# Level masks moved from GpSimd to VectorE, and reciprocal roots computed by a power instruction on GpSimd, in a two-layer encoder trunk

## The chip, the cores and the metric

The kernel runs on one core of one Trainium2 chip. The metric is the device time of one launch in microseconds (us); the time given is the median of three runs. The core has the matrix engine TensorE (PE in the profile), VectorE (DVE), ScalarE (ACT), GpSimd (POOL), and SyncE (SP), which here only issues DMAs. All engines run their own instruction streams and meet at semaphores.

## What is computed

Two layers over one sequence of 256 tokens of width 2048, all in fp32. Every layer is a token mixer and a SwiGLU feed-forward part, each closed by a residual sum and a LayerNorm. The mixer of layer 0 has two halves, RWKV-7 (16 heads of 64, both directions) and gated linear attention (GLA, 4 heads); that of layer 1 is differential attention. Reciprocal square roots stand in five places:

```python
def _layer_norm(x, g, b, eps=1e-5):
    mu = mean(x); var = mean(square(x - mu))
    return (x - mu) * rsqrt(var + eps) * g + b        # 4 times over D=2048; and per RWKV head (eps 64e-5)

def _rms_norm(x, g, eps=1e-5):                        # GLA output (256 wide), attention output (128 wide)
    return x * rsqrt(mean(x*x) + eps) * g

def _l2norm(t, eps=1e-12):                            # RWKV: kk = _l2norm(heads(k * k_k)), per token and head
    return t / maximum(sqrt(sum(t*t)), eps)

def step(S, inp):                                     # RWKV-7, one token; the kernel does it in chunks of 64
    r_t, w_t, k_t, v_t, kk_t, a_t = inp
    sa = -einsum(S, kk_t)
    S = S * w_t + sa * (kk_t * a_t) + v_t * k_t
    return S, einsum(S, r_t)
```

## The kernel before, in words

The large projections multiply in split fp32: ScalarE copies a weight tile to a rounded high part (`high`), VectorE subtracts for the low part (`low`), and TensorE runs three matmuls for each product. One wait counter for each pair of producer and consumer sets the order; there is no scheduler, each engine's block is written out by hand.

The RWKV half runs over 8 pairs of heads (`PAIRS`), one after the other, the sequence cut into 4 chunks of 64 in both directions (8 units). For each pair, the inverse of a triangular 64 x 64 matrix for each unit is built by doubling, in levels `lv` 1 to 5. At each level TensorE makes three products (`L1984`): Q = V * C into PSUM `py`, then the new V into `pt` and the new W into `pa`. ScalarE copies the upper 64 partitions of each into SBUF and VectorE the lower 64: Q into `R_Qbd` (L1338, L1648), V into `R_Vbd` (L1342, L1652), W into `R_wc` (L1346, L1656). TensorE's next product waits for both copies. C of a level is the score matrix `R_G` times that level's 0/1 mask, written by `level(eng, lv)` (L250, L255), in two instructions of 64 x 512. VectorE does levels 0 and 1, GpSimd levels 2 to 5, each as soon as the buffer `R_C[lv % 2]` is free (`q_done` two levels back). After the levels comes a serial chain over 4 chunks, then `pair_done`.

Work for the next pair is spread into the gaps of the levels. The tables `ACT_AT`, `DVE_AT`, `PE_AT` say which numbered piece of `next_act`, `next_dve`, `next_pe` stands at which level and point (0 is behind the Q copy, 1 behind the V copy, 2 behind the W copy). VectorE's piece 3 clamps the sum of squares of kk into `R_sh[:, 1]` (L1578, 128 x 256, semaphore `ss_clamped`). ScalarE turns it into the reciprocal root with Ln (piece 3, L1287) and Exp with scale -0.5 (piece 4, L1290), semaphore `rn_ready`, for which VectorE's piece 4 waits at L1587. Ln, Exp and Sigmoid do not share a loaded table here, so a table load stands ahead of each change.

The tail of a pair, a LayerNorm over each head, lies at the start of the next pair: VectorE computes four variances (`ys_var`, L1691), ScalarE does Ln and Exp on 128 x 4 (`act_tail`, L1301, L1303), VectorE normalises (`normed`, L1599) and later finishes (`finish`, L1606 to L1611). GpSimd, per pair: zeroes `R_UV`, copies the next z columns (`next_z`), copies `R_Kbd` and `R_Rbd`, does the four masks, then `next_factors`. The other reciprocal roots are L1405/L1407 (each GLA head, 128 x 2), L1472/L1474 (attention, 128 x 32, once) and `end_act` (L669/L671, 128 x 2, four times).

## Time and profile before

| | us |
|---|---|
| median of 3 runs | 3432.48 (3430.94 to 3436.76) |
| the profiled execution | 3431.72 |
| its span | 3429.9 |
| PE busy | 2875.8 (84%) |
| DVE busy | 2180.7 (64%) |
| ACT busy | 1216.6 (35%) |
| POOL busy | 364.4 (11%) |
| chain that ended last, by engine | PE 63%, issue 16%, DVE 13%, DVEq 4%, ACT 2%, ACTq 1% |

The profile gives the busy time of each engine, the groups of instructions by line (L255 is line 255 of the kernel), the idle time ahead of each group with what ended it, and single instructions in order of time. The projections and feed-forward parts take most of the span; the RWKV pairs lie between about 452 and 1040 us, the GLA heads after them to 1166 us, the attention heads between 2392 and 2509 us.

### The profile page before, as it was taken

The numbers are of one execution on the slowest core, as the hardware profiler recorded it, in microseconds if no ns is written. First come the engines' busy times: TensorE is split into PE (matmuls) and PEld (weight loads), VectorE is DVE, ScalarE is ACT, GpSimd is POOL, SyncE is SP. The second block draws the span as 40 slices with busy tenths as digits, with TensorE's granted clock in tenths as the row PEclk, the third lists the DMA queues.
The fourth block names the chain that finished last, engine by engine and source line by source line (L and its number), as shares of the span: only waits on it lengthen the run. The fifth ranks groups of instructions, "written<-read, shape, count | busy, mean of one in ns | idle before, by whom it ended". The sixth has DMA issues, their size and how long they took to land.

```text
span 3429.9 us, 43071 instructions
## 1 busy us (share of the span) xinstructions
PE 2875.8 (84%) x16704; PEld 2381.3 (69%) x16704; DVE 2180.7 (64%) x2308; ACT 1216.6 (35%) x1398; POOL 364.4 (11%) x405
## 2 busy tenths in 40 slices
PE   1799857776773588999999996999678899999996
PEld 1588746666662476888888885887556788888885
DVE  7768355666655656777778778743666555555557
ACT  0333333333323343333333332433543333333332
POOL 0000042333220002000000002011801000000001
PEclk9999967667675698999999997999778999999998
DMA  9799410110004454888678873955034555555552
GB/s 357 277 348 357 140 32 29 38 45 28 28 1 160 172 164 154 325 311 318 258 298 329 304 280 114 356 179 171 0 111 135 175 193 184 195 188 191 187 192 86
DMA packets 256765, 635.48 MB, mean 185 GB/s; under 512 B 10238, under 2 KB 17204, under 8 KB 234292
## 3 DMA queue, kind: packets, MB, share of 16 engines
q1 hardware_dynamic: 250530, 621.77, 51.0%
q10 hardware_dynamic: 6162, 12.72, 1.0%
q8 instruction: 48, 0.79, 0.1%
q14 instruction: 25, 0.20, 0.0%
HBM read 632.35 MB, written 2.10 MB: 185 GB/s over the span
## 4 chain that ended last, share of the span: by engine, by line
PE 63%; issue 16%; DVE 13%; DVEq 4%; ACT 2%; ACTq 1%; DMA 0%; POOL 0%; POOLq 0%; SPq 0%
PE pa L552 9%; PE pa L554 9%; PE pa L553 9%; PE pb L552 5%; PE pb L554 5%; PE pb L553 5%; PE py L552 4%; PE py L554 4%; PE py L553 4%; DVE s_wl L462 2%; PE pt L1984 1%; DVE s_wide L501 1%; DVE s_htl L607 1%; PE pa L1984 1%; PE pt L511 1%
## 5 line engine op out<-in xcount | busy, mean ns | idle before, releaser
L462 DVE TENSOR_TENSOR s_wl<-s_raw,s_wh 128x2048 fp32r<-128x2048 f32 (+1 forms) x396 | 919.4, 2323 | 709.5 <-ACT s_wh L457 707.3
L457 ACT ACTIVATE s_wh<-s_raw 128x2048 fp32r<-128x2048 f32 (+1 forms) x396 | 757.8, 1915 | 1300.7 <-PE pa L554 638.9
L552 PE MATMUL pa<-s_wh,s_hth 128*128 128x512 f32 (+1 forms) x1760 | 703.3, 400 | 48.9 <-DVE s_wl L462 33.0
L553 PE MATMUL pa<-s_wl,s_hth 128*128 128x512 f32 (+1 forms) x1760 | 695.4, 395 | 0.0
L554 PE MATMUL pa<-s_wh,s_htl 128*128 128x512 f32 (+1 forms) x1760 | 694.5, 395 | 0.0
L552 PEld LDWEIGHTS pa<-s_wh,s_hth 128*128 128x128 f32 x1760 | 337.9, 192 | 125.7 <-issue 46.3
L554 PEld LDWEIGHTS pa<-s_wh,s_htl 128*128 128x128 f32 x1760 | 337.1, 192 | 71.4
L553 PEld LDWEIGHTS pa<-s_wl,s_hth 128*128 128x128 f32 x1760 | 337.9, 192 | 68.5
L501 DVE SCALAR_TENSOR_TENSOR s_wide<-s_adaw,s_silu_c,s_wide 128x2048 f32<-128x2048 f32 x150 | 352.7, 2351 | 4.2 <-issue 3.0
L552 PE MATMUL py<-s_wh,s_guh 128*128 128x512 f32 x704 | 278.1, 395 | 13.3 <-DVE s_ysum L913 10.8
L554 PE MATMUL py<-s_wh,s_gul 128*128 128x512 f32 x704 | 276.0, 392 | 0.0
L553 PE MATMUL py<-s_wl,s_guh 128*128 128x512 f32 x704 | 275.8, 392 | 0.0
L552 PE MATMUL pb<-s_wh,s_hth 128*128 128x512 f32 x704 | 274.5, 390 | 0.0
L553 PE MATMUL pb<-s_wl,s_hth 128*128 128x512 f32 x704 | 273.9, 389 | 0.0
L554 PE MATMUL pb<-s_wh,s_htl 128*128 128x512 f32 x704 | 273.9, 389 | 0.0
L552 PEld LDWEIGHTS py<-s_wh,s_guh 128*128 128x128 f32 x704 | 133.5, 190 | 46.8 <-DVE s_wl L462 8.4
L554 PEld LDWEIGHTS py<-s_wh,s_gul 128*128 128x128 f32 x704 | 133.3, 189 | 28.2
L553 PEld LDWEIGHTS py<-s_wl,s_guh 128*128 128x128 f32 x704 | 133.6, 190 | 27.5
L552 PEld LDWEIGHTS pb<-s_wh,s_hth 128*128 128x128 f32 x704 | 132.2, 188 | 27.5 <-DVE s_wl L462 0.3
L554 PEld LDWEIGHTS pb<-s_wh,s_htl 128*128 128x128 f32 x704 | 132.1, 188 | 27.4
L553 PEld LDWEIGHTS pb<-s_wl,s_hth 128*128 128x128 f32 x704 | 132.2, 188 | 27.2
L719 POOL TENSOR_TENSOR s_xt<-s_xt,s_lng 128x2048 f32<-128x2048 f32 x6 | 28.9, 4830 | 805.6 <-PE py L580 792.8
(339 smaller groups left out, 3166.8 us busy)
## 6 DMA issues: line engine op xcount, KB each, us to landing
s_raw<-in_ffn_w_in SPq DMA_DIRECT2D x176, 1024.0 KB, 5.2
...
```

Source lines behind the costliest of these rows:

```text
L457: act.activation(wh[:, s % 2, :, 0:width], raw[:, s, :, 0:width], ACT.Copy).then_inc(hi_done, 1)
L462: dve.tensor_tensor(wl[:, s % 2, :, 0:width], raw[:, s, :, 0:width], wh[:, s % 2, :, 0:width].bitcast(F32), ALU.subtract).then_inc(lo_done, 1)
L501: dve.scalar_tensor_tensor(wide[:], adaw[:, slot], silu_c[:, bass.ds(k, 1)], wide[:], ALU.mult, ALU.add).then_inc(ada_step, 1)
L511: mm = pe.matmul(bank[:, m:m + 1], wide[:, m * P:(m + 1) * P], ones[:, 0:1], start=(m == 0), stop=True, skip_group_check=True)
L552: pe.matmul(o, a_hi, w_hi, start=start and k == 0, stop=False)
L553: pe.matmul(o, a_hi, w_lo, start=False, stop=False)
L554: mm = pe.matmul(o, a_lo, w_hi, start=False, stop=stop and k == UK - 1)
L607: dve.tensor_tensor(htl[:, 2 * g:2 * g + 2, :], htmp[:, g % 2], hth[:, 2 * g:2 * g + 2, :].bitcast(F32), ALU.subtract).then_inc(h_lo, 1)
L719: pool.tensor_tensor(xt[:, i], xt[:, i], lng[:], ALU.mult)
L1984: mm = pe.matmul(bank[r, h, u * CH:(u + 1) * CH], lhs(u, h), rhs(u, h), start=(start or (start is None and u == 0)), stop=True, skip_group ...
```

## The change

1. `level` is called for levels 2 to 5 by VectorE, between its Q copy and its V copy, and no longer by GpSimd.
2. Every reciprocal root is one `tensor_tensor` with `ALU.pow` on GpSimd, its second operand a column that holds -0.5, broadcast. ScalarE's Ln and Exp for it go, with the pieces 3 and 4 of `next_act`; the pieces left are numbered anew in `ACT_AT`.
3. The factor 65536 inside Ln and the factor 256 behind it go, so that L1587 becomes a plain product.

```diff
--- before.py
+++ after.py
@@ -250,8 +250,6 @@
         def level(eng, lv):
 
             for h, rows_ in enumerate((slice(0, CH), slice(CH, P))):
-                if h and eng is nc.gpsimd:
-                    eng.drain()
                 ins = eng.tensor_tensor(
                     R_C[rows_, lv % 2].rearrange("p (d c) n -> p d c n", d=2),
                     R_G[rows_, h, :, 0:CH].rearrange("p (d c) n -> p d c n", d=2),
@@ -277,7 +275,7 @@
         IN_PARTS = {c: 4 * (c - 1) if c < 5 else 4 * (c - 2) for c in (1, 2, 3, 4, 6, 7, 8, 9)}
 
 
-        ACT_AT = {(1, 2): 1, (2, 0): 2, (3, 2): 3, (4, 0): 4, (4, 1): 5, (4, 2): 6}
+        ACT_AT = {(1, 2): 1, (2, 0): 2, (4, 1): 3, (4, 2): 4}
         DVE_AT = {(1, 0): 0, (1, 2): 1, (2, 2): 2, (3, 0): 3, (4, 1): 4}
         PE_AT = {1: 1, 2: 2}
 
@@ -664,12 +662,6 @@
             act.dma_start(lng[:], ln_g[n // 2, n % 2].partition_broadcast(P)).then_inc(ln_in, 16)
             act.dma_start(lnb[:], ln_b[n // 2, n % 2].partition_broadcast(P)).then_inc(ln_in, 16)
 
-        def end_act(act, n):
-            act.wait_ge(end_var, n + 1)
-            act.activation(small[:, 36:38], small[:, 34:36], ACT.Ln)
-            act.drain()
-            act.activation(small[:, 38:40], small[:, 36:38], ACT.Exp, scale=-0.5).then_inc(end_rstd, 1)
-
         stats = small[:, 40:88].rearrange("p (i c s) -> p i c s", i=NT, s=6)
 
         def end_block(dve, n, q):
@@ -1098,6 +1090,8 @@
         @block.gpsimd
         def _(pool):
             pool.memset(rows[:], 0.0).then_inc(rows_zero, 1)
+            pool.memset(small[:, 95:96], -0.5)
+            half_neg = small[:, 95:96]
 
             pool.wait_ge(unit_done, 2 + 4 * ABC)
             for tile in (R_Kbd, R_Rbd, R_Wbd, R_Qbd, R_Vbd):
@@ -1122,6 +1116,12 @@
             def units(tile, rows_, at):
                 return tile[rows_, :, at:at + CH]
             full, top, low_half = slice(0, P), slice(0, CH), slice(CH, P)
+
+            def next_norm(n):
+
+                pool.wait_ge(ss_clamped, n + 1)
+                pool.sem_inc(passed, 1)
+                pool.tensor_tensor(R_sh[:, 1], R_sh[:, 1], half_neg.to_broadcast((P, SEQ)), ALU.pow).then_inc(rn_ready, 1)
 
             def next_factors(n):
 
@@ -1136,9 +1136,17 @@
                     pool.tensor_tensor(units(R_AB, rows_, at_b), both(R_rk[rows_, 1]), R_e2[rows_], ALU.mult)
                 pool.drain().then_inc(ab_ready, 1)
 
-            def pool_pair(t, more):
+            def pool_tail(t):
+
+                pool.wait_ge(ys_var, t + 1)
+                pool.sem_inc(passed, 1)
+                pool.tensor_tensor(small[:, 24:28], small[:, 16:20], half_neg.to_broadcast((P, 4)), ALU.pow).then_inc(ys_rstd, 1)
+
+            def pool_pair(t, more, tail=True):
                 pool.wait_ge(pair_done, t + 1)
                 pool.sem_inc(passed, 1)
+                if tail:
+                    pool_tail(t - 1)
                 pool.memset(R_UV[:], 0.0)
                 pool.drain().then_inc(init_ready, 1)
                 if more:
@@ -1151,20 +1159,19 @@
                 pool.tensor_copy(R_Kbd[CH:P, :, CH:P], R_KR[CH:P, :, 0:CH])
                 pool.tensor_copy(R_Rbd[CH:P, :, CH:P], R_KR[CH:P, :, CH:P])
                 pool.drain().then_inc(krbd_ready, 1)
-                for lv in range(2, LEVELS):
-                    pool.wait_ge(first_ready if lv == 2 else q_done, t + 1 if lv == 2 else t * (LEVELS - 1) + lv - 2)
-                    pool.sem_inc(passed, 1)
-                    level(pool, lv)
-                    pool.drain().then_inc(c_ready, 1)
                 if more:
+                    next_norm(t + 1)
                     pool.wait_ge(ab_turned, t + 1)
                     pool.sem_inc(passed, 1)
                     next_factors(t + 1)
             next_z(0)
+            next_norm(0)
             next_factors(0)
-            with pool.Fori(0, PAIRS - 1) as t:
+            pool_pair(0, True, False)
+            with pool.Fori(1, PAIRS - 1) as t:
                 pool_pair(t, True)
             pool_pair(PAIRS - 1, False)
+            pool_tail(PAIRS - 1)
             pool.wait_ge(tail_done, PAIRS)
             pool.sem_inc(passed, 1)
 
@@ -1180,16 +1187,29 @@
                 pool.drain().then_inc(gv_ready, 1)
             gla_qk(0)
             gla_v(0)
+            def gla_norm(n):
+                pool.wait_ge(g_var, n)
+                pool.sem_inc(passed, 1)
+                pool.tensor_tensor(small[:, 32:34], small[:, 28:30], half_neg.to_broadcast((P, 2)), ALU.pow).then_inc(g_rstd, 1)
             with pool.Fori(1, GH) as n:
                 pool.wait_ge(g_turned, n)
                 pool.sem_inc(passed, 1)
                 gla_qk(n)
                 pool.wait_ge(g_o, n)
                 pool.sem_inc(passed, 1)
+                gla_norm(n)
                 gla_v(n)
+            gla_norm(GH)
+
+            def end_norm(n):
+
+                pool.wait_ge(end_var, n + 1)
+                pool.tensor_tensor(small[:, 38:40], small[:, 34:36], half_neg.to_broadcast((P, 2)), ALU.pow).then_inc(end_rstd, 1)
+            end_norm(0)
             pool.wait_ge(x_ready, 2)
             pool.memset(ysum[:], 0.0).then_inc(ysum_zero, 1)
             end_pool(pool, 0)
+            end_norm(1)
             end_pool(pool, 1)
 
             pool.wait_ge(pa_free, 2 + 2 * (17 + FG + 8))
@@ -1201,9 +1221,13 @@
                     pool.wait_ge(at_turned, m * 2 + (slot - 1))
                     pool.sem_inc(passed, 1)
                     rotate(pool, m * 2 + slot, slot)
+            pool.wait_ge(at_var, 1)
+            pool.tensor_tensor(A_rs[:], A_ss[:], half_neg.unsqueeze(1).to_broadcast((P, NT, DH)), ALU.pow).then_inc(at_rstd, 1)
+            end_norm(2)
             pool.wait_ge(x_ready, 6)
             pool.memset(ysum[:], 0.0).then_inc(ysum_zero, 1)
             end_pool(pool, 2)
+            end_norm(3)
             pool.wait_ge(ln_in, 4 * 32)
             pool.wait_ge(x_ready, 8)
             pool.sem_inc(passed, 1)
@@ -1283,28 +1307,13 @@
                     act.activation(R_lw[:, 2], pb[:, 1, 0:SEQ], ACT.Sigmoid, bias=tab[:, bass.ds(n + (T_W0 + 16), 1)])
                     act.activation(R_gn[:], pb[:, 1, SEQ:W], ACT.Copy).then_inc(up_act, 1)
                 elif piece == 3:
-                    act.wait_ge(ss_clamped, n + 1)
-                    act.activation(R_sh[:, 1], R_sh[:, 1], ACT.Ln, scale=65536.0)
-                    act.drain()
-                elif piece == 4:
-                    act.activation(R_sh[:, 1], R_sh[:, 1], ACT.Exp, scale=-0.5).then_inc(rn_ready, 1)
-                elif piece == 5:
                     act.wait_ge(logs_ready, n + 1)
                     act.activation(R_e1[:], R_b[:], ACT.Exp)
                     act.activation(R_e2[:], R_b[:], ACT.Exp, scale=-1.0)
                 else:
                     act.activation(R_lw[:, 0:2], R_lw[:, 0:2], ACT.Exp).then_inc(exps_ready, 1)
 
-            def act_tail(t):
-
-                act.wait_ge(ys_var, t + 1)
-                act.activation(small[:, 20:24], small[:, 16:20], ACT.Ln)
-                act.drain()
-                act.activation(small[:, 24:28], small[:, 20:24], ACT.Exp, scale=-0.5).then_inc(ys_rstd, 1)
-
             def act_pair(t, more, tail=True):
-                if tail:
-                    act_tail(t - 1)
                 act.wait_ge(pair_done, t + 1)
                 act.wait_ge(exps_ready, t + 1)
                 act.activation(R_dec[:, 0], R_e1[:, 0].rearrange("p (c n) -> p c n", n=CH)[:, :, CH - 1], ACT.Copy)
@@ -1355,13 +1364,12 @@
                     act.wait_ge(u_done[1], t * NCH + i + 1)
                     act.activation(R_UV[0:CH, 0, u], py[0:CH, 1, 0:CH], ACT.Copy, scale=-1.0)
                     act.activation(R_UV[CH:P, 1, u], py[CH:P, 1, 0:CH], ACT.Copy, scale=-1.0).then_inc(u_ready[1], 1)
-            for piece in range(7):
+            for piece in range(5):
                 next_act(0, piece)
             act_pair(0, True, False)
             with act.Fori(1, PAIRS - 1) as t:
                 act_pair(t, True)
             act_pair(PAIRS - 1, False)
-            act_tail(PAIRS - 1)
 
             for i in range(NT):
                 act.activation(z[:, i, Z_OG:Z], z[:, i, Z_OG:Z], ACT.Silu).then_inc(og_ready, 1)
@@ -1401,10 +1409,6 @@
                 act.drain().then_inc(g_sq, 1)
                 if more:
                     gla_next_ln(t + 1)
-                act.wait_ge(g_var, t + 1)
-                act.activation(small[:, 30:32], small[:, 28:30], ACT.Ln)
-                act.drain()
-                act.activation(small[:, 32:34], small[:, 30:32], ACT.Exp, scale=-0.5).then_inc(g_rstd, 1)
             gla_next_act(0)
             gla_next_ln(0)
             with act.Fori(0, GH - 1) as t:
@@ -1417,12 +1421,10 @@
             out_act(act, 13, 13, 0)
             high(act, C_FFN0, 0)
             high(act, C_FFN0, 1)
-            end_act(act, 0)
             turn_act(act, 1)
             ffn_act(act, C_FFN0, 0, 17, 1)
             high(act, C_DIFF, 0)
             high(act, C_DIFF, 1)
-            end_act(act, 1)
             turn_act(act, 2)
             in_act(act, C_DIFF, qkv)
 
@@ -1468,20 +1470,14 @@
             exps(0, 0, first=True)
             heads(act, act_head)
             act.drain().then_inc(at_sq, 1)
-            act.wait_ge(at_var, 1)
-            act.activation(A_ss[:], A_ss[:], ACT.Ln)
-            act.drain()
-            act.activation(A_rs[:], A_ss[:], ACT.Exp, scale=-0.5).then_inc(at_rstd, 1)
             for m in range(DH // 2):
                 act.wait_ge(at_scaled, m + 1)
                 act.activation(hth[:, 2 * m:2 * m + 2], A_t2[:, m % 2], ACT.Copy).then_inc(at_hi, 1)
             out_act(act, C_OUT1, 17 + FG + 12, 2)
             high(act, C_FFN1, 0)
             high(act, C_FFN1, 1)
-            end_act(act, 2)
             turn_act(act, 3)
             ffn_act(act, C_FFN1, FG, n_of[FG], 3)
-            end_act(act, 3)
 
         @block.vector
         def _(dve):
@@ -1584,7 +1580,7 @@
                     dve.drain()
                     dve.tensor_tensor(R_rk[:, 1], R_rk[:, 1], R_sh[:, 2], ALU.mult)
                     dve.wait_ge(rn_ready, n + 1)
-                    dve.scalar_tensor_tensor(R_kk[:], R_kk[:], 256.0, R_sh[:, 1], ALU.mult, ALU.mult)
+                    dve.tensor_tensor(R_kk[:], R_kk[:], R_sh[:, 1], ALU.mult)
                     dve.drain()
                     dve.tensor_tensor(R_sh[:, 0], R_kk[:], R_lw[:, 2], ALU.mult)
                     dve.scalar_tensor_tensor(R_sh[:, 1], R_rk[:, 0], tab[:, bass.ds(n + T_RK, 1)], R_rk[:, 1],
@@ -1648,6 +1644,7 @@
                     dve.tensor_copy(R_Qbd[low_half, :, CH:P], tiles(py, 1)).then_inc(qc_ready, 1)
                     ahead(lv, 0)
                     if lv < LEVELS - 1:
+                        level(dve, lv + 1).then_inc(c_ready, 1)
                         dve.wait_ge(v_done, t * (LEVELS - 1) + lv + 1)
                         dve.tensor_copy(R_Vbd[low_half, :, CH:P], tiles(pt, 1)).then_inc(vc_ready, 1)
                         ahead(lv, 1)
```

The first place is ScalarE's stream in the loop over the pairs, from the Q copy of level 3 (L1338 before, L1347 now) to the two Exps of the next pair's decay (`R_e`) at level 4. First before:

```order
L1338 ACTIVATE s_R_Qbd<-py 64x8x64
L1341 REGISTER_ALU
L1342 ACTIVATE s_R_Vbd<-pt 64x8x64
L1346 ACTIVATE s_R_wc<-pa 64x512
L1287 ACT_TABLE_LOAD
L1287 ACTIVATE s_R_sh<-s_R_sh 128x256
L1338 ACTIVATE s_R_Qbd<-py 64x8x64
L1290 ACT_TABLE_LOAD
L1290 ACTIVATE s_R_sh<-s_R_sh 128x256
L1341 REGISTER_ALU
L1342 ACTIVATE s_R_Vbd<-pt 64x8x64
L1293 ACTIVATE s_R_e<-s_R_b 128x512
```

and now:

```order
L1347 ACTIVATE s_R_Qbd<-py 64x8x64
L1350 REGISTER_ALU
L1351 ACTIVATE s_R_Vbd<-pt 64x8x64
L1355 ACTIVATE s_R_wc<-pa 64x512
L1347 ACTIVATE s_R_Qbd<-py 64x8x64
L1350 REGISTER_ALU
L1351 ACTIVATE s_R_Vbd<-pt 64x8x64
L1311 ACT_TABLE_LOAD
L1311 ACTIVATE s_R_e<-s_R_b 128x512
L1312 ACTIVATE s_R_e<-s_R_b 128x512
```

Ln with its load behind level 3's W copy is gone; the load for Exp now stands between the V copy and the W copy of level 4, and the Exp that made the root is gone.

The second place is VectorE's stream in the same loop, from the Q copy of level 3 to the V copy of level 4. Before:

```order
L1648 COPY s_R_Qbd<-py 64x8x64
L1578 TENSOR_SCALAR s_R_sh<-pb 128x256
L1580 TENSOR_TENSOR s_R_lw<-s_R_b,s_R_lw 128x512
L1651 REGISTER_ALU
L1652 COPY s_R_Vbd<-pt 64x8x64
L1656 COPY s_R_wc<-pa 64x512
L1648 COPY s_R_Qbd<-py 64x8x64
L1651 REGISTER_ALU
```

and now:

```order
L1644 COPY s_R_Qbd<-py 64x8x64
L1574 TENSOR_SCALAR s_R_sh<-pb 128x256
L1576 TENSOR_TENSOR s_R_lw<-s_R_b,s_R_lw 128x512
L253 TENSOR_TENSOR s_raw<-s_R_G,s_cst 64x512 x2
L1648 REGISTER_ALU
L1649 COPY s_R_Vbd<-pt 64x8x64
L1653 COPY s_R_wc<-pa 64x512
L1644 COPY s_R_Qbd<-py 64x8x64
L253 TENSOR_TENSOR s_raw<-s_R_G,s_cst 64x512 x2
L1648 REGISTER_ALU
```

Two mask instructions (L253, `s_raw` holds `R_C`) stand ahead of each V copy; the piece with the clamp (L1574 now) stands ahead of them.

The third place is GpSimd's stream in the loop, one pair. Before, from the copies of `R_Kbd` and `R_Rbd` (`s_xt` holds their source):

```order
L1148 COPY s_R_Kbd<-s_xt 64x8x64
L1149 COPY s_R_Rbd<-s_xt 64x8x64
L1151 COPY s_R_Kbd<-s_xt 64x8x64
L1152 COPY s_R_Rbd<-s_xt 64x8x64
L255 TENSOR_TENSOR s_raw<-s_R_G,s_cst 64x512 x2
L1155 ISA
L255 TENSOR_TENSOR s_raw<-s_R_G,s_cst 64x512 x2
L1155 REGISTER_ALU
L255 TENSOR_TENSOR s_raw<-s_R_G,s_cst 64x512 x2
L1155 REGISTER_ALU
L255 TENSOR_TENSOR s_raw<-s_R_G,s_cst 64x512 x2
L1128 REGISTER_ALU
```

and now, from the tail's power on:

```order
L1143 TENSOR_TENSOR s_small<-s_small 128x4
L1150 MEMSET s_R_UV 128x1024
L1110 ISA
L1110 COPY s_R_zs<-s_z 128x384
L1110 ISA
L1110 COPY s_R_zs<-s_z 128x384
L1156 COPY s_R_Kbd<-s_xt 64x8x64
L1157 COPY s_R_Rbd<-s_xt 64x8x64
L1159 COPY s_R_Kbd<-s_xt 64x8x64
L1160 COPY s_R_Rbd<-s_xt 64x8x64
L1122 REGISTER_ALU
L1124 TENSOR_TENSOR s_R_sh<-s_R_sh,s_small 128x256
```

The four masks are gone. A power on 128 x 4 (L1143) stands ahead of the zeroing of `R_UV`, and a power on 128 x 256 (L1124) ahead of the factors.

## Rows read from the trace of the kernel before

**Rows 1.** Busy time by engine, PEclk, DMA share, GB/s, over the RWKV pairs.
```profile
452.00:1040.00 588.00, 420.79 (x5739) 368.68 (x5740) 354.14 (x694) 202.66 (x422) 186.79 (x170) 0.71 0.08 29
```

**Rows 2.** VectorE in time: start, duration, instruction, idle time before and its releaser.
```profile
623.77 1.52 DVE L1552 TENSOR_TENSOR s_R_sh<-s_R_zf 128x768 f32<-128x768 f32 x1
625.47 1.65 DVE L1555 TENSOR_SCALAR s_R_sh<-s_R_sh,s_hmu 128x256 f32<-128x256 f32 x3 [0.17 <-issue]
...
630.11 1.07 DVE L1566 TENSOR_SCALAR s_R_kk<-s_R_rk,s_tab 128x256 f32<-128x256 f32 x1 [0.22 <-issue]
631.25 1.46 DVE L1568 TENSOR_TENSOR s_R_sh<-s_R_kk 128x256 f32<-128x256 f32 x1
632.74 0.70 DVE L1648 COPY s_R_Qbd<-py 64x512 f32<-64x512 f32 x1
635.60 0.69 DVE L1652 COPY s_R_Vbd<-pt 64x512 f32<-64x512 f32 x1 [2.16 <-PE pt L1984]
...
642.02 0.69 DVE L1652 COPY s_R_Vbd<-pt 64x512 f32<-64x512 f32 x1
...
643.97 0.69 DVE L1648 COPY s_R_Qbd<-py 64x512 f32<-64x512 f32 x1 [0.32 <-PE py L1984]
648.19 0.69 DVE L1652 COPY s_R_Vbd<-pt 64x512 f32<-64x512 f32 x1 [3.53 <-PE pt L1984]
...
676.56 2.90 DVE L1599 TENSOR_SCALAR s_R_Vbd<-s_R_y,s_R_mv,s_small 64x64 f32<-64x64 f32 x8 [1.82 <-ACT s_small L1303]
...
687.27 1.39 DVE L255 TENSOR_TENSOR s_raw<-s_R_G,s_cst 64x512 f32<-64x512 f32 x2
...
689.97 1.22 DVE L1609 TENSOR_TENSOR s_R_y<-s_R_y,s_R_bonus 128x256 f32<-128x256 f32 x1
691.39 1.24 DVE L1611 TENSOR_TENSOR s_xt<-s_R_y,s_R_g 128x256 f32 x1 [0.20 <-issue]
```

**Rows 3.** VectorE by shape, 430 to 450 us: count, busy, mean ns, idle.
```profile
L1552 DVE TENSOR_TENSOR s_R_sh<-s_R_zf 128x768 f32<-128x768 f32 x1 | 1.0, 957 | 6.1 <-ACT s_R_zf L1274 6.1
...
L1555 DVE TENSOR_SCALAR s_R_sh<-s_R_sh,s_hmu 128x256 f32<-128x256 f32 x3 | 0.9, 348 | 0.1
...
L1568 DVE TENSOR_TENSOR s_R_sh<-s_R_kk 128x256 f32<-128x256 f32 x1 | 0.4, 427 | 0.1
...
L1566 DVE TENSOR_SCALAR s_R_kk<-s_R_rk,s_tab 128x256 f32<-128x256 f32 x1 | 0.4, 353 | 0.1
```

**Rows 4.** VectorE in time, before the first pair.
```profile
451.82 1.29 DVE L498 TENSOR_SCALAR s_wide<-s_adaw,s_silu_c 128x2048 f32<-128x2048 f32 x1 [0.19 <-issue]
453.21 3.19 DVE L501 SCALAR_TENSOR_TENSOR s_wide<-s_adaw,s_silu_c,s_wide 128x2048 f32<-128x2048 f32 x1
```

**Rows 5.** GpSimd in time, same stretch.
```profile
452.13 2.12 POOL L1131 TENSOR_TENSOR s_xt<-s_R_kk,s_R_lw 128x512 f32<-128x512 f32 x1 [15.06 <-ACT s_R_lw L1296]
454.20 3.33 POOL L1132 TENSOR_TENSOR s_xt<-s_R_rk,s_R_e 128x512 f32<-128x512 f32 x1
```

**Rows 6.** TensorE in time, behind a pair's first products.
```profile
693.40 1.11 PE L1930 MATMUL pb<-s_cst,s_R_zs 128*128 128x128 f32 x6 [0.23 <-DVE s_R_bonus L1636]
```

**Rows 7.** ScalarE in time, level 3 of one pair.
```profile
643.56 1.28 ACT L1287 ACT_TABLE_LOAD   x1
...
645.44 0.59 ACT L1338 ACTIVATE s_R_Qbd<-py 64x512 f32<-64x512 f32 x1 [0.17 <-issue]
```

**Rows 8.** GpSimd by shape, whole span.
```profile
L784 POOL TENSOR_TENSOR s_wide<-s_wide 128x128 f32<-128x128 f32 x32 | 18.4, 595 | 2.4 <-issue 0.2
```

**Rows 9.** GpSimd in time, behind the first LayerNorm.
```profile
1298.42 9.62 POOL L719 TENSOR_TENSOR s_xt<-s_xt,s_lng 128x2048 f32<-128x2048 f32 x2 [6.39 <-issue]
```

**Rows 10.** VectorE by shape, the GLA heads.
```profile
L1767 DVE SCALAR_TENSOR_TENSOR s_L_o<-pa,s_small,s_z 128x256 f32<-128x256 f32 x8 | 3.5, 480 | 10.4 <-ACT s_small L1407 10.4
```

**Rows 11.** VectorE in time, behind the attention heads.
```profile
2509.29 1.66 DVE L1854 TENSOR_SCALAR s_A_on<-s_qkv,s_A_rs 128x128 f32<-128x128 f32 x8 [2.98 <-ACT s_A_rs L1474]
```

**Rows 12.** VectorE in time, behind the last LayerNorm's variance.
```profile
3411.33 2.98 DVE L709 TENSOR_SCALAR s_xt<-s_xt,s_small 128x1024 f32<-128x1024 f32 x4 [1.82 <-ACT s_small L671]
```

## The prediction, written before the changed kernel was run

> **What bounds the kernel now.** I read first the busy shares and the chain that ended last: 84% TensorE, and DVE with its queue 17%, so the projections run at TensorE's pace and the change does not touch them beyond four small roots. Then the busy times of stretches. Between 452 and 1040 us, where the eight RWKV pairs run, no engine is full: in 588 us TensorE is busy 421 at a granted clock of 0.71, VectorE 354, ScalarE 203, GpSimd 187 [rows 1]. A stage like that is bound by waits, so I read one pair (623 to 697 us; 588 us over eight pairs is some 73 each) instruction by instruction on each engine, looking for the place where each handover comes last. Three kinds of place matter. One: VectorE itself is last, with no idle time before its copy, as at the V copy of level 3 and the Q copy of level 2 (642.02 and 632.74, [rows 2]). Two: VectorE waits, 2.16 us for level 2's V and 3.53 us for level 4's [rows 2], so more work fits. Three: ScalarE is last, with its Q copy of level 3 at 645.44 where VectorE's began at 643.97 [rows 2, 7], because a table load of 1.28 us and Ln stand ahead of it; and with the tail's root, for which VectorE idles 1.82 us [rows 2].
>
> The same rows show a cost that no wait names. VectorE's instructions with two SBUF inputs, and its one-input `tensor_scalar`, are longer while GpSimd works: L1552 1.52 us against 0.96, the three L1555 1.65 against about 0.9, L1566 1.07 against 0.35, L1568 1.46 against 0.43 [rows 2, 3]. The stretch before the first pair shows how: VectorE's L498 begins at 451.82 and ends at 453.11, GpSimd's L1131 begins at 452.13 and lasts until 454.25 although alone such a one takes far less; VectorE's L501 begins at 453.21 and takes 3.19 us, of which 2.15 lie behind that end, and GpSimd's next takes 3.33 [rows 4, 5]. They take turns, each a whole instruction long.
>
> The Trainium skill has this as a rule (SBUF — State Buffer, Who interferes with whom): a VectorE instruction in a two-port mode or with two SBUF inputs and a GpSimd instruction that reads SBUF exclude each other for the whole instruction. The trace agrees, by the turns just read. By that rule a long GpSimd instruction is not hidden beside VectorE merely because nobody waits for its result.
>
> **The change, part by part.** Terms are for one pair, negative is time gained.
>
> Masks, gone from GpSimd. Their turns go with them. In the finish of the tail, L1609 and L1611 (1.22 and 1.24 us, alone 0.43 like L1568) lose 1.6 us [rows 2, 3]. Behind them stand a bonus product, the two masks of level 1 and a V copy, so far until about 695.2 (691.39 + 1.24 + 0.43 + 1.39 + 0.69 and the gaps), and TensorE's next product waits for them. 1.6 us less and TensorE is late instead: its transposes L1930 run from 693.40 for 1.11 us after a wait of 0.23 [rows 6], so it is free at about 694.3. Gain 1.0.
> In level 1 (623.77 to 632.74) the excess of L1552, L1555, L1566 and L1568 is 0.56 + 0.75 + 0.72 + 1.03 = 3.1 us, all on the path.
>
> Masks, added to VectorE: two of 64x512 take 1.39 us [rows 2], four times a pair. Level 2's stands in level 1 where VectorE is last: 1.4, so this stretch nets 1.4 - 3.1 = -1.7. Level 3's falls in the idle 2.16, level 5's in the idle 3.53: 0. Level 4's stands ahead of the V copy at 642.02, which waited for nothing: +1.4. Gone cover would cost 1.4 each.
>
> Ln and its load, gone from level 3: ScalarE's Q copy may start with VectorE's, 645.44 - 643.97 = 1.5 us earlier [rows 2, 7]. TensorE's next products wait for both. Gain 1.5. The load for Exp remains, now behind the V copy of level 4 and ahead of ScalarE's W copy; it delays its Q copy of level 5 by 1.28 less what VectorE's piece 4 keeps TensorE waiting anyway: between 0 and 1.3, taken 0.3.
>
> The tail's root: 1.82 us idle [rows 2] become a power on 128x4 with two semaphore crossings. An ordinary product on GpSimd of 128x128 takes 0.595 us and of 128x2048 4.81 [rows 8, 9]: 2.2 ns an element above a fixed 0.31. With 0.3 for the crossings (my estimate, about double what 1.82 leaves beside the load, Ln and Exp) it is 0.6 us. Gain 1.2. GpSimd now zeroes and copies after it, beside VectorE's `normed` and the two L501, and takes turns with them: 0 to some four turns of 0.6, taken 0.4. ScalarE's copies into `R_UV` start later, but what TensorE makes of them it needs only behind VectorE's level 0 masks (687.27) [rows 2]: 0.
>
> The root of kk, a power on 128x256, call its length p. The clamp stands ahead of the V copy of level 3 (642.02) and L1587, which wants the root, behind that of level 4 (648.19): over 6 us apart, some 8 with level 4's masks between them [rows 2]. So a root with p under 8 comes in time. Its turn is the question. The clamp releases it while L1580 (two SBUF inputs) is about to start; GpSimd takes the turn behind L1580, and the two masks of level 4 wait for its end. V copy and TensorE stand behind those. So I charge +p in full. Nothing in the trace shows a power. From below it costs one ordinary product: 0.31 + 256 x 2.2 ns = 0.9 us. From above I take the largest GpSimd row, 9.62 us for 2 x 2048 elements [rows 9], sixteen ordinary passes. A power is at least a logarithm, a product and an exponential, three passes: 0.31 + 3 x 0.56 = 2.0 us. I take 2.0, which is near the lower end and to the rows of like shape.
>
> Sum for a pair: -1.0 - 1.7 + 1.4 - 1.5 + 0.3 - 1.2 + 0.4 = -3.3, plus p. There are seven pairs with a next pair's pieces and seven with a tail before them: -23.1 + 7p. The last pair's masks fall beside TensorE's products: 0. Before the first pair the same root is on the path with ScalarE's Ln and Exp so far; VectorE's one-input instructions behind it would wait for the turn: +1.0 once.
>
> GLA: ahead of L1767 VectorE idles 10.4 us in four waits (x8 are two a head) [rows 10]; each becomes 0.6, so 8.0 less; GpSimd's copies of the next head move behind the root into VectorE's two-input work, 0.3 each for three heads: -7.1. Loads of Exp stay, but fall ahead of a wait.
> Attention: 2.98 us idle [rows 11] become 0.3 + 0.31 + 32 x 6.6 ns = 0.8: -2.2. Last LayerNorm: 1.82 [rows 12] become 0.6: -1.2. The three inner LayerNorms' roots lay beside two `low` subtractions and still do: 0, at most one turn each way. The new load ahead of the Exp of lambda falls beside a DMA: 0.
>
> The Trainium skill prices a table switch at about 2.66 us, the load and a drain of 1.38 (ScalarE: Activation LUTs, What ACT_TABLE_LOAD costs). The trace disagrees: Ln, load, Exp and both crossings together fit in 1.82 us. By the page each switch that leaves the path would give 1.4 us more, some 25 us over the kernel; the sum stays with the rows.
>
> Total: -23.1 - 7.1 - 2.2 - 1.2 + 1.0 = -32.6, plus 7p. With p = 2.0 that is -18.6. The profiled execution took 3431.72 us (span 3429.90, 1.8 outside), 0.8 under the median of 3432.48. 3431.7 - 18.6 = 3413.
>
> **The rivals.** A measurement of this kernel can tell about 0.2%, 6.9 us, from no change.
>
> A, slow power: the power needs tens of cycles an element, and level 4's masks wait for all of it. Price 7p; equal at p = 4.7, slower by more than 6.9 us from p = 5.6. At 9.6 us: 3431.7 - 32.6 + 67 = 3466. For it: nothing bounds a transcendental on an engine that needs 2.2 ns for a product. Against it: nothing in the trace. Between 3.7 and 5.6 the result is within 0.2%.
>
> B, the power takes no turn or lets VectorE through, since it computes more than it reads: then only its latency counts and 8 us hide it: 3431.7 - 32.6 = 3399. Against it: ordinary GpSimd instructions held VectorE for all their length.
>
> C, the masks cost what they say and the turns give nothing back, because other waits were just behind: gains 1.0 and 3.1 of a pair vanish, 28.7 us: 3413 + 29 = 3442. Against it: VectorE shows no idle time in these stretches.
>
> D, the change leaves the loads in place and the path as it was: of five loads a pair two remain in the instruction order, so this can only be part true.
>
> **How the numbers follow.** Forecast (p from 0.9 to 3.7, turns as said) 0.50, at 3413, its own range 3404 to 3425. A beyond p = 5.6 has 0.23, the stretch between 0.09; B 0.10; C 0.08, a quarter of it within 0.2%. Faster by over 0.2%: 0.50 + 0.10 = 0.60. Within: 0.09 + 0.02 = 0.11. Slower: 0.23 + 0.06 = 0.29. The range goes from B, 3397, to a power of about 8 us, 3456.
>
> **What would show it.** The row of L1124 gives p; level 4's first mask (L253) on VectorE is longer by about p, against 0.7. L1552, L1568, L1609, L1611 should fall to 0.96 and 0.43. VectorE's wait ahead of `normed` should read 0.5 to 0.7 instead of 1.82, that ahead of the GLA head's scaling (L1767 before) about 0.6. A pair should take 1.3 us less than its 73. I am wrong if the masks of level 4 are short beside a running power (then B), if p is above 4, or if TensorE's clock in the pairs leaves 0.71 by more than 0.03: 0.03 of it on 421 busy us is 18 us, as much as my whole gain.

## The result, and the profile after

The changed kernel takes 3675.17 us (median of 4 runs, 3669.83 to 3679.38) against 3431.71 for the kernel before (4 runs): a ratio of 1.072, 95% interval 1.0705 to 1.0736. It is 243 us slower. The forecast was 3413 with a range up to 3456. The profiled execution took 3669.83 us, its span 3667.9.

VectorE in time shows a pair's levels 3 and 4 (start, duration, instruction, idle time before it and its releaser), the stretch that answers to [rows 2] from 640 us on:

```profile
636.51 0.42 DVE L1574 TENSOR_SCALAR s_R_sh<-pb 128x256 f32<-128x256 f32 x1
637.03 0.69 DVE L1576 TENSOR_TENSOR s_R_lw<-s_R_b,s_R_lw 128x512 f32<-128x512 f32 x1
637.64 1.80 DVE L253 TENSOR_TENSOR s_raw<-s_R_G,s_cst 64x512 f32<-64x512 f32 x2
639.47 0.69 DVE L1649 COPY s_R_Vbd<-pt 64x512 f32<-64x512 f32 x1
...
642.14 1.39 DVE L253 TENSOR_TENSOR s_raw<-s_R_G,s_cst 64x512 f32<-64x512 f32 x2
...
644.66 0.42 DVE L1581 TENSOR_TENSOR s_R_rk<-s_R_rk,s_R_sh 128x256 f32<-128x256 f32 x1
678.74 0.42 DVE L1583 TENSOR_TENSOR s_R_kk<-s_R_kk,s_R_sh 128x256 f32<-128x256 f32 x1 [33.65 <-POOL s_R_sh L1124]
```

The clamp (L1574) starts the power; the masks of level 4 (637.64) and level 5 (642.14) run beside it; then VectorE sits idle for 33.65 us until the power is done. GpSimd and TensorE in the same stretch:

```profile
637.12 41.59 POOL L1124 TENSOR_TENSOR s_R_sh<-s_R_sh,s_small 128x256 f32<-128x256 f32 x1 [25.82 <-DVE s_R_sh L1574]
```

```profile
643.21 1.13 PE L1981 MATMUL pa<-s_R_wc,s_R_Qbd 128*64 128x64 f32 x32
644.20 1.15 PE L1981 MATMUL py<-s_R_Vbd,s_raw 128*64 128x64 f32 x32
681.63 1.98 PE L1981 MATMUL pa<-s_R_wc,s_R_Qbd 128*64 128x64 f32 x32 [36.28 <-DVE s_R_Qbd L1644]
```

One power on 128x256 lasts 41.59 us. TensorE waits with VectorE, because VectorE's W copy of level 4 and Q copy of level 5 are queued behind L1583, and its next product takes 1.98 us where the two before took 1.13 and 1.15. By shape (count, busy us, mean ns, idle before), first the powers on GpSimd, then VectorE's instruction that wants the root of kk:

```profile
L1124 POOL TENSOR_TENSOR s_R_sh<-s_R_sh,s_small 128x256 f32<-128x256 f32 x8 | 332.6, 41579 | 184.3 <-DVE s_R_sh L1574 184.3
...
L1143 POOL TENSOR_TENSOR s_small<-s_small 128x4 f32<-128x4 f32 x8 | 8.1, 1008 | 171.3 <-DVE s_small L1688 171.3
...
L1225 POOL TENSOR_TENSOR s_A_rs<-s_A_ss,s_small 128x32 f32<-128x32 f32 x1 | 5.4, 5425 | 18.1 <-DVE s_A_ss L1842 18.1
...
L1207 POOL TENSOR_TENSOR s_small<-s_small 128x2 f32<-128x2 f32 x4 | 2.8, 703 | 1752.7 <-DVE s_small L691 1752.7
```

```profile
L253 DVE TENSOR_TENSOR s_raw<-s_R_G,s_cst 64x512 f32<-64x512 f32 x96 | 68.7, 716 | 2.7
...
L1583 DVE TENSOR_TENSOR s_R_kk<-s_R_kk,s_R_sh 128x256 f32<-128x256 f32 x8 | 3.4, 425 | 275.4 <-POOL s_R_sh L1124 275.4
```

275.4 us of waiting in eight places, 39.92 of them once before the first pair, is more than the whole loss of 243. So the rest of the change must have gained about 32. Its small terms can be read too. Busy times over the RWKV part, with as many of TensorE's matmuls (5741) as in [rows 1] (5739); it now takes 836 us where [rows 1] had 588:

```profile
452.00:1288.00 836.00, 420.03 (x5741) 368.90 (x5740) 365.72 (x764) 166.88 (x372) 461.77 (x122) 0.63 0.06 20
```

The tail's normalisation waits 1.22 us instead of 1.82, the attention scaling 5.54 instead of 2.98 ([rows 11]), and the instructions that had taken turns with GpSimd's masks are at their lengths of [rows 3] again:

```profile
602.42 3.00 DVE L1595 TENSOR_SCALAR s_R_Vbd<-s_R_y,s_R_mv,s_small 64x64 f32<-64x64 f32 x8 [1.22 <-POOL s_small L1143]
...
616.03 0.42 DVE L1605 TENSOR_TENSOR s_R_y<-s_R_y,s_R_bonus 128x256 f32<-128x256 f32 x1
616.66 0.42 DVE L1607 TENSOR_TENSOR s_xt<-s_R_y,s_R_g 128x256 f32 x1 [0.20 <-issue]
...
621.90 0.96 DVE L1548 TENSOR_TENSOR s_R_sh<-s_R_zf 128x768 f32<-128x768 f32 x1
623.03 0.88 DVE L1551 TENSOR_SCALAR s_R_sh<-s_R_sh,s_hmu 128x256 f32<-128x256 f32 x3 [0.17 <-issue]
...
2747.60 1.66 DVE L1851 TENSOR_SCALAR s_A_on<-s_qkv,s_A_rs 128x128 f32<-128x128 f32 x8 [5.54 <-POOL s_A_rs L1225]
```

For a ledger of a pair I took VectorE's copy of `R_y` and its five Q copies as marks in each trace; a stretch runs from one mark's start to the next. Means in us over the six pairs that prepare a next one and have a tail before them (five in waited96). The columns beside before and after are experiments told below.

| stretch | before | after | masks_only | small_only | kk_at_back | masks45 | waited96 |
|---|---|---|---|---|---|---|---|
| `R_y` to Q 1 | 23.60 | 21.88 | 22.25 | 23.17 | 21.61 | 23.60 | 22.09 |
| Q 1 to Q 2 | 9.69 | 7.83 | 7.83 | 9.65 | 7.83 | 7.93 | 7.83 |
| Q 2 to Q 3 | 7.00 | 5.88 | 5.86 | 6.84 | 5.48 | 6.26 | 6.90 |
| Q 3 to Q 4 | 4.49 | 5.63 | 5.21 | 4.48 | 5.21 | 5.21 | 5.36 |
| Q 4 to Q 5 | 6.92 | 39.38 | 5.80 | 6.52 | 5.67 | 6.07 | 14.15 |
| Q 5 to `R_y` | 21.58 | 22.41 | 22.01 | 21.60 | 22.42 | 22.04 | 22.42 |
| sum | 73.28 | 103.01 | 68.96 | 72.26 | 68.22 | 71.11 | 78.75 |

The loss stands in one stretch, Q 4 to Q 5, where the root is awaited. The five others together are 2.7 us shorter than before.

### The profile page after: what moved, and what is told of

Read it like the earlier page. It is cut to its first block and busy times, and to the rows that moved or that the text cites. A ratio compares the mean times of both kernels' runs of the same rounds, so it can differ in the third digit from the quotient of the medians.

```text
span 3667.9 us, 42876 instructions
## 1 busy us (share of the span) xinstructions
PE 2873.2 (78%) x16704; PEld 2379.2 (65%) x16704; DVE 2188.1 (60%) x2372; ACT 1157.4 (32%) x1311; POOL 652.6 (18%) x367
## 5 line engine op out<-in xcount | busy, mean ns | idle before, releaser
L1124 POOL TENSOR_TENSOR s_R_sh<-s_R_sh,s_small 128x256 f32<-128x256 f32 x8 | 332.6, 41579 | 184.3 <-DVE s_R_sh L1574 184.3
L1981 PE MATMUL pa<-s_R_wc,s_R_Qbd 128*64 128x64 f32 x1280 | 52.4, 242 | 254.7 <-DVE s_R_Qbd L1644 254.7
L1981 PEld LDWEIGHTS pa<-s_R_wc,s_R_Qbd 128*64 128x64 f32 x1280 | 48.5, 157 | 255.6 <-DVE s_R_wc L1653 254.6
L1583 DVE TENSOR_TENSOR s_R_kk<-s_R_kk,s_R_sh 128x256 f32<-128x256 f32 x8 | 3.4, 425 | 275.4 <-POOL s_R_sh L1124 275.4
```

What stands on the lines that cost most here:

```text
L1124: pool.tensor_tensor(R_sh[:, 1], R_sh[:, 1], half_neg.to_broadcast((P, SEQ)), ALU.pow).then_inc(rn_ready, 1)
L1583: dve.tensor_tensor(R_kk[:], R_kk[:], R_sh[:, 1], ALU.mult)
L1981: mm = pe.matmul(bank[r, h, u * CH:(u + 1) * CH], lhs(u, h), rhs(u, h), start=(start or (start is None and u == 0)), stop=True, skip_group ...
```

## The experiments

**kk_back and kk_at_back: the long roots back on ScalarE.** kk_back undoes one part of the change, the root of kk:

```diff
-        ACT_AT = {(1, 2): 1, (2, 0): 2, (4, 1): 3, (4, 2): 4}
+        ACT_AT = {(1, 2): 1, (2, 0): 2, (3, 2): 3, (4, 0): 4, (4, 1): 5, (4, 2): 6}
...
-                    next_norm(t + 1)
...
                 elif piece == 3:
+                    act.wait_ge(ss_clamped, n + 1)
+                    act.activation(R_sh[:, 1], R_sh[:, 1], ACT.Ln, scale=65536.0)
+                    act.drain()
+                elif piece == 4:
+                    act.activation(R_sh[:, 1], R_sh[:, 1], ACT.Exp, scale=-0.5).then_inc(rn_ready, 1)
```

kk_at_back puts the attention's root (128x32) back on ScalarE as well.

> The changed kernel with one part undone: the 128x256 root of kk is back on ScalarE (Ln behind the W copy of level 3, Exp behind the Q copy of level 4, factors 65536 and 256 restored). Theory L (the whole loss is the latency of the 41.6 us power, which VectorE awaits at L1583 in seven loops and before the first pair): the time falls from 3675 to below the time before. By the terms of the prediction without those of the kk root (-1.0 -1.7 +1.4 for the masks and -1.2 +0.4 for the tail root, times seven, GLA -7.1, last LayerNorm -1.2) and with the attention root at what its row shows (5.43 us of power for 2.98 us of wait, +2.8): 3431.7 - 23.0 + 2.8 = 3411, between 3400 and 3422. Rival T (GpSimd's powers hold VectorE, or the masks on VectorE cost more than they gain, so that a part of the 243 us is not the wait): the time stays above 3440.

> As the one before, and the attention root (128x32) is back on ScalarE too; GpSimd keeps the powers on 128x4 and 128x2, VectorE the masks. If the attention power's wait is what its row shows, it is 2 to 4 us faster than the kernel with that power: 3431.7 - 23.0 = 3409. If short powers beside VectorE hurt by contention and not by their length, no difference.

kk_back took 3396.66 us, ratio to before 0.9907 (0.9892 to 0.9922); kk_at_back 3390.19, 0.989 (0.9875 to 0.9905). Against the changed kernel kk_back is 278.5 us faster by the medians (their runs were made at different times), and the waits for the power had summed to 275.4: the one 128x256 instruction is the whole loss, to within a few us. Both are also below the 3411 and 3409 of the expectation, so the rest gains more than was thought. The attention wait went from 5.54 us back to 2.98 in the trace; the medians differ by 6.5, but their intervals overlap, so only the 2.6 of the trace is shown.

**masks_only and small_only: each other part alone.** masks_only is the kernel before with

```diff
+                        level(dve, lv + 1).then_inc(c_ready, 1)
                         dve.wait_ge(v_done, t * (LEVELS - 1) + lv + 1)
```

on VectorE and GpSimd's loop over levels 2 to 5 gone. small_only is the kernel before with only the powers on 128x4 and 128x2.

> The kernel before with the masks of levels 2 to 5 on VectorE and nothing else; all roots stay on ScalarE. The prediction's mask terms (-1.0 -1.7 +1.4 a pair, seven pairs): -9.1, so 3422.6. Rival C (mask turns give nothing back because other waits stand just behind, masks cost 1.4 a pair or more): 3441 or more. Rival N (the idle time takes all): no change within 0.2%.

> The kernel before with only the small roots as powers on GpSimd: 128x4 of the tail, 128x2 of the GLA heads and of the LayerNorms; masks stay on GpSimd, roots of kk and attention on ScalarE. The prediction's terms: tail 7 x (-1.2 +0.4) = -5.6, GLA -7.1, last LayerNorm -1.2, sum -13.9: 3417.8. By the rows of the changed kernel (waits of 1.22 ahead of the tail's normalisation and 0.9 in GLA instead of 0.6) the tail gives 7 x 0.2 and GLA about 5: 3424. Rival: the table loads that stay on ScalarE move onto the path, then no gain.

masks_only: 3399.12 us, ratio 0.9915 (0.9899 to 0.9931), 27 us under the 3426.18 of before in the same runs, three times the 9.1 expected. small_only: 3422.00, ratio 0.9983 (0.9974 to 0.9993), 4 us, and the expectation from the changed kernel's rows (3424, or 8 down) was nearer than the prediction's 13.9. In GLA the wait ahead of the scaling fell from 10.4 to 3.9 us as foreseen, but from the first head's scaling to the last's it is 75.0 us instead of 78.0, so of 1.6 us less wait a head 1.0 arrives; what takes the rest is open.

**idle_power, idle_products and idle_power_top: does a running power hold VectorE?** To kk_at_back one power is added that nobody awaits, released by the clamp as the real one was:

```diff
+                pool.wait_ge(ss_clamped, n + 1)
+                pool.sem_inc(passed, 1)
+                pool.tensor_tensor(scr[:, 0:32], scr[:, 0:32], half_neg.to_broadcast((P, 32)), ALU.pow)
```

idle_products has six drained products of 128x256 there; idle_power_top has the power on 64 partitions x 64 columns.

> The kernel with the roots of kk and attention on ScalarE, the masks on VectorE and the short powers on GpSimd (3390), to which one power on 128x32 is added on GpSimd, released by the clamp of kk as the 128x256 power was; its result goes to a buffer that nobody reads or awaits. Its length should be the 5.4 us of the attention power. Rule of turns (my prediction: VectorE's level 4 masks wait for all of it): +5.4 a pair, seven pairs, about 3428, and the first mask's row above 5 us. Rival L (only the latency of an awaited power counts): within 5 us of 3390, the mask pair at most 0.4 us longer than its 1.39, as beside the 41.6 us power.

> As idle_power, but instead of the power six ordinary products of 128x256 with two SBUF inputs stand there on GpSimd, drained one by one, about as long together (6 x 0.9 = 5.4 us). If ordinary products hold VectorE's two-input instructions and a power does not, the masks here are longer, by about one product each (0.9 us), +1.8 a pair and 13 us in all: about 3403. If products too pass beside the masks: within 5 us of 3390.

> As idle_power (a power on GpSimd that nobody awaits), on 64 partitions x 64 columns in place of 128 x 32, the same number of elements. If the length goes by columns (0.38 + 0.161 each): 10.7 us. If it goes by elements: 5.9 us, as before. The time stays at 3390 to 3396 in either case.

Times: 3395.33 (ratio 0.9907, 0.9873 to 0.994), 3390.84 (0.99, 0.9862 to 0.9937) and, one run, 3393.34 us, none of them to be told from kk_at_back. The 3403 expected of idle_products did not come: its masks cost 0.74 us a pair, as said below, which is 5 us in all and less than its runs differ among themselves (3386 to 3402). VectorE's level 4 masks, first in kk_at_back, then beside the power of 32 columns, beside that on 64x64, and beside the products:

```profile
629.65 1.38 DVE L253 TENSOR_TENSOR s_raw<-s_R_G,s_cst 64x512 f32<-64x512 f32 x2
```

```profile
633.05 1.43 DVE L254 TENSOR_TENSOR s_raw<-s_R_G,s_cst 64x512 f32<-64x512 f32 x2
```

```profile
636.91 1.48 DVE L254 TENSOR_TENSOR s_raw<-s_R_G,s_cst 64x512 f32<-64x512 f32 x2
```

```profile
633.49 2.12 DVE L254 TENSOR_TENSOR s_raw<-s_R_G,s_cst 64x512 f32<-64x512 f32 x2
```

and what stood on GpSimd meanwhile, in idle_power, idle_products and idle_power_top in turn:

```profile
632.53 5.87 POOL L1126 TENSOR_TENSOR s_scr<-s_scr,s_small 128x32 f32<-128x32 f32 x1 [24.33 <-DVE s_R_sh L1584]
```

```profile
632.97 5.38 POOL L1126 TENSOR_TENSOR s_scr<-s_cst,s_small 128x256 f32<-128x256 f32 x6 [24.32 <-DVE s_R_sh L1585]
```

```profile
L1126 POOL TENSOR_TENSOR s_scr<-s_scr,s_small 64x64 f32<-64x64 f32 x8 | 87.8, 10974 | 186.4 <-DVE s_R_sh L1584 186.4
```

Beside 5.87 us of power the pair of masks is 0.05 us longer than 1.38; beside 5.38 us of products it is 0.74 longer, about one product (mean 770 ns). So the turn is real for ordinary instructions and one long; a power does not hold VectorE for its length. It does hold it a little, and by its columns: in every one of these kernels the masks begin 0.52 us behind the power, and the pair takes 1.43, 1.48, 1.53 and 1.80 us beside powers of 32, 64, 96 (waited96, below) and 256 columns (the changed kernel). That is 0.0016 us a column, 0.42 us for a power of 41.59; level 5's masks, which run beside that same power 4.5 us later, take their 1.39 again. What the power does in that first part no run shows. And the power's price goes by columns: 10.97 us for 64 columns on half the partitions, 5.87 for 32 on all.

**waited96: an awaited power of another length.** As idle_power with 96 columns, and VectorE waits for it and for ScalarE's root:

```diff
-                    dve.wait_ge(rn_ready, n + 1)
+                    dve.wait_ge(rn_ready, n * 2 + 2)
```

> As idle_power with a power on 128x96, and VectorE awaits it where it awaits the root of kk. By the row of 128x256 and 128x32 (41.6 and 5.4 us, so 0.161 us a column and 0.3 fixed) it takes 15.8 us. Theory L: wait = length less the cover of 7.9 us (41.58 - 33.65, a pair of the changed kernel): 7 x 7.9 = 55, and before the first pair, where almost nothing covers it, about 14: 3459. Rule of turns (the masks wait for all of it, so 7 x 15.8 + 14 = 125): 3515.

3475.00 us, ratio 1.0136 (1.0102 to 1.0171): 85 above kk_at_back's 3390, between the 69 of theory L and the 125 of turns. The wait is what L says:

```profile
669.10 1.53 DVE L254 TENSOR_TENSOR s_raw<-s_R_G,s_cst 64x512 f32<-64x512 f32 x2
...
684.70 0.42 DVE L1593 SCALAR_TENSOR_TENSOR s_R_kk<-s_R_kk,s_R_sh 128x256 f32<-128x256 f32 x1 [8.41 <-POOL s_scr L1126]
```

and the same line's eight waits by shape:

```profile
L1593 DVE SCALAR_TENSOR_TENSOR s_R_kk<-s_R_kk,s_R_sh 128x256 f32<-128x256 f32 x8 | 3.4, 426 | 73.5 <-POOL s_scr L1126 73.5
```

The power takes 16.08 us (mean of eight), less 8.41 of wait leaves 7.7 covered, and all eight waits are 73.5. Most of the other 11 are in another stretch, Q 2 to Q 3, 1.4 us a pair longer than in kk_at_back. TensorE's two products there are longer. In time, waited96 first, then kk_at_back:

```profile
661.16 1.98 PE L1991 MATMUL pt<-s_R_Qbd,s_R_wc 128*64 128x64 f32 x32 [2.40 <-DVE s_R_Qbd L1654]
662.89 1.80 PE L1991 MATMUL pa<-s_R_wc,s_R_Qbd 128*64 128x64 f32 x32
```

```profile
623.16 1.15 PE L1981 MATMUL pt<-s_R_Qbd,s_R_wc 128*64 128x64 f32 x32 [2.40 <-DVE s_R_Qbd L1644]
624.11 1.13 PE L1981 MATMUL pa<-s_R_wc,s_R_Qbd 128*64 128x64 f32 x32
```

and the two stretches by engine (columns as in [rows 1]; the sixth number behind the length is the granted clock), in the same order:

```profile
661.10:664.70 3.60, 3.54 (x65) 3.50 (x65) 2.01 (x3) 0.59 (x1) 0.00 (x0) 0.54 0.00 0
```

```profile
623.10:625.30 2.20, 2.14 (x65) 2.11 (x66) 1.95 (x4) 0.61 (x2) 0.00 (x0) 1.00 0.00 0
```

A clock of 0.54 is near the lower level, 1.2 GHz, 1.00 the upper, 2.4. Right ahead of both stands the same idle time of 2.40 us, so the last wait alone does not decide the level. Nor is it the kernel that decides: in the changed kernel's own trace, behind 2.2 to 2.4 us of idle time, this first product takes 1.98 us in one pair, 1.48 in one and 1.15 in five.

**masks45: where the masks' unforeseen gain comes from.** The kernel before with only the masks of levels 4 and 5 on VectorE (`if lv > 2:` ahead of the added `level(dve, lv + 1)`, and `range(2, 4)` in GpSimd's loop).

> The kernel before with only the masks of levels 4 and 5 on VectorE; GpSimd keeps levels 2 and 3, ScalarE all roots. Gone are the turns of L1566 and L1568 in the level 1 stretch, 0.72 + 1.03 = 1.75 a pair. By the prediction's term, level 4's masks ahead of the V copy of level 3 then cost 1.4 and level 5's nothing: -0.35 x 7 = -2.5, no change against 3426. Theory K (VectorE's later copies cost less than they take, because ScalarE's Q copy of level 4 stands behind a table load and Ln anyway, and TensorE, which waits less long, then works at its faster level): the stretch from Q copy 3 to Q copy 5, 4.49 + 6.92 = 11.41 us before, shrinks to about 11.0 in place of growing to 12.8, so 1.75 + 0.4 = 2.1 a pair and 15 us in all: 3411.

3412.10 us, ratio 0.9949 (0.9931 to 0.9967): 17.5 under before, near K's 15, far from no change. In the ledger Q 1 to Q 2 loses 1.76 (1.75 expected), and Q 3 to Q 5 goes from 11.41 to 11.28, where the term of 1.4 for level 4's masks would have made it 12.8. Two things stand against that term, as rows of masks_only show beside the kernel before. Before, ScalarE's Q copy of level 4 began 1.47 us behind VectorE's (645.44 against 643.97, [rows 2, 7]); with the masks VectorE's is later and ScalarE's no more, 0.24 behind:

```profile
635.69 1.28 ACT L1280 ACT_TABLE_LOAD   x1
636.99 0.42 ACT L1280 ACTIVATE s_R_sh<-s_R_sh 128x256 f32<-128x256 f32 x1
637.57 0.59 ACT L1331 ACTIVATE s_R_Qbd<-py 64x512 f32<-64x512 f32 x1 [0.17 <-issue]
```

```profile
637.33 0.69 DVE L1641 COPY s_R_Qbd<-py 64x512 f32<-64x512 f32 x1 [0.65 <-PE py L1978]
```

And TensorE, which waits 1.02 us there instead of 2.25, runs that product in 1.15 us instead of 1.98. First the kernel before, its row in time and its stretch by engine with the clock, then the same two of masks_only:

```profile
646.18 1.98 PE L1984 MATMUL pt<-s_R_Qbd,s_R_wc 128*64 128x64 f32 x32 [2.25 <-ACT s_R_Qbd L1338]
```

```profile
646.10:649.90 3.80, 3.72 (x74) 3.75 (x76) 1.60 (x4) 3.34 (x6) 0.00 (x0) 0.55 0.00 0
```

```profile
638.31 1.15 PE L1978 MATMUL pt<-s_R_Qbd,s_R_wc 128*64 128x64 f32 x32 [1.02 <-ACT s_R_Qbd L1331]
```

```profile
638.30:640.40 2.10, 2.08 (x64) 1.95 (x64) 2.00 (x4) 2.09 (x4) 0.00 (x0) 1.00 0.00 0
```

That pair is one of two kinds, and the pairs of the ledger separate the clock from the masks. In the kernel before three of the six have this product at the lower level (1.93 to 1.98 us) and take 11.8 us from Q 3 to Q 5; three have it at 1.15 and take 11.0 to 11.2. masks45 has two of the first kind (11.81), although TensorE waited no longer there (1.02 us) than in those, and four of the second (11.0 to 11.2); masks_only has only the second (11.0 to 11.2). So at equal clock the masks of levels 4 and 5 cost nothing here and gain nothing: VectorE's Q copy comes 0.2 us later and ScalarE's is 0.2 us less behind it (0.23 instead of 0.43 in most of these pairs). The lower level costs 0.8 us, and 11.41 to 11.28 is one pair fewer at it.

The largest unforeseen gain is elsewhere, in Q 2 to Q 3: 1.14 us in masks_only, 0.74 in masks45, which has no new mask there. In the kernel before, level 2's first two products run wholly or in part at the lower level in all six pairs, behind 4.25 us of idle time. With VectorE free of the turns ahead of them the idle time is 2.4 to 2.5, and the stretch is 5.48 in the pairs where these products ran at the upper level throughout (four of six in masks_only, one in masks45) and 6.2 to 7.0 in the others. So this gain is the clock's; that the shorter idle time brought it is likely and not shown, since both levels occur behind 2.4 us.

**split3: a candidate.** kk_at_back with the subtraction of piece 3 (0.69 us ahead of level 4's masks and V copy) moved behind the W copy of level 3 (`(3, 2): 5` in `DVE_AT`).

> Candidate: the kernel with kk and attention roots on ScalarE; the subtraction of piece 3 (128x512, 0.69 us with its gap, ahead of level 4's masks and the V copy, for which TensorE waits) moves behind the W copy of level 3, with a drain ahead of it. If this V copy is what TensorE waits for there (it waits 1.09 us for it with the masks on VectorE), each pair gains 0.6 and the kernel 4: 3386. If the next wait is just behind (VectorE's Q copy of level 4): no change, 3390.

3390.55 us, ratio 0.9885 (0.985 to 0.992): no change. Q 3 to Q 4 falls from 5.21 to 4.59 and Q 4 to Q 5 rises from 5.67 to 6.30. TensorE waits less for the V copy (0.30 instead of 1.09) and then longer for ScalarE's Q copy (1.71 instead of 0.92), which stands behind the table load and Ln that the same clamp releases:

```profile
635.47 1.15 PE L1982 MATMUL py<-s_R_Vbd,s_raw 128*64 128x64 f32 x32 [0.30 <-DVE s_R_Vbd L1650]
638.33 1.15 PE L1982 MATMUL pt<-s_R_Qbd,s_R_wc 128*64 128x64 f32 x32 [1.71 <-ACT s_R_Qbd L1343]
```

The version to keep is kk_at_back: masks on VectorE, powers only on 128x4 and 128x2, 0.989 of the time before (0.9875 to 0.9905), and 285 us under the changed kernel by the medians. The two parts alone gained 27 and 4 us against its 36; the 5 between are not accounted for.

## Why the prediction was wrong, point by point

- **The length of the power, the step that failed.** "From above I take the largest GpSimd row, 9.62 us ... I take 2.0." The power is 41.58 us, 4 times the upper bound and 20 times the value taken. The bound was another instruction's length, not a bound: no row showed a power, and counting "three passes" assumed that its steps cost what a product costs. By the measured lengths (41.58, 16.08 and 5.87 us for 256, 96 and 32 columns) it is 0.16 us a column and less than 1 us fixed; one of 2 columns is 0.70, one of 4 is 1.01. Rival A said in words that nothing bounds a transcendental on that engine, and then priced it with 9.6 too.
- **What it costs the path, also wrong, and hidden by the first.** "GpSimd takes the turn behind L1580, and the two masks of level 4 wait for its end. V copy and TensorE stand behind those. So I charge +p in full." They took 1.80 us instead of 1.38 beside 41.59 us of power, and 1.43 beside 5.87. Rival B, given 0.10, had the mechanism: only latency counts. Its "8 us hide it" measured 7.9 (41.58 less 33.65) and 7.7 in waited96. So the loss is (41.6 - 7.9) x 7 + 39.9 = 276 us. By the same rows a p of 2.0 would have cost nothing in the pairs, where the sum charged 14 us for it. Before the first pair, where nothing covers it, the sum put 1.0 and the wait is 39.9. So with the right length the forecast's own sum, 3431.7 - 32.6 + 7 x 41.6 = 3690, would have come near the measured 3675 by luck: it charges 7 x 7.9 = 55 us that are hidden and leaves out 39 that are not.
- **The rule of turns.** The rule of the Trainium skill (SBUF — State Buffer, Who interferes with whom), exclusion for the whole instruction, agrees with [rows 4, 5] and with idle_products (0.74 us for a product of 0.77). The power breaks it: 5.87 us cost 0.05 and 41.59 cost 0.42. Here the measurement decides.
- **Masks gone from GpSimd.** Terms -1.0 and -1.7 (with the mask added) in the first two stretches: measured -1.35 and -1.86 in masks_only. Right to 0.35 us. (By its own row TensorE is free at 693.40 + 1.11 = 694.5 and not at 694.3, which would have made the first term -0.7.)
- **Masks on VectorE.** "+1.4" for level 4 measured +0.72 in its stretch, and "0" for levels 3 and 5 measured -1.14 and -1.12. The term -1.3 a pair was -4.3. Failed as a size: the profile gave VectorE's own time, but the stretch belongs to the latest of three engines and to TensorE's clock. At equal clock Q 3 to Q 5 is 11.0 to 11.2 us with these masks and without, and the gain from Q 2 to Q 3 is the clock's alone.
- **"Ln gone: gain 1.5".** Mostly counted twice. Once the masks delay VectorE's Q copy, ScalarE's is only 0.24 us behind it in masks_only, with Ln still there, and TensorE waits 1.02 us; in the changed kernel, with Ln gone beside the same masks, the two copies start together and it waits 0.89. Taking Ln out at no cost elsewhere was not run. (That copy is level 4's; the prediction called it level 3's.)
- **Small roots.** The tail's wait is 1.22 where 0.6 was said (the power is 1.01, my estimate 0.3): in small_only its own stretch, `R_y` to Q 1, loses 0.43 us a pair against 0.8 said. The sum of a pair loses 1.0, but the rest is in stretches where no small root stands and where the same two kinds of pair occur, so that agreement is luck. GLA's waits are 3.9 us in all instead of 2.4. The last LayerNorm waits 0.83, not 0.6. Attention was said to gain 2.2 and loses 2.6, since a power on 32 columns is 5.4 us and not 0.5. That too is the power's price.
- **The clock.** "I am wrong if ... TensorE's clock in the pairs leaves 0.71 by more than 0.03": it fell to 0.63. That is a consequence of the wait: in kk_at_back, without it, the RWKV part (452 to 1007 us) has 0.70.
